# Matrix-LSTM key blocks: masks added in place on DMA-fetched row copies, DVE one block ahead of its own weighing

## The chip, the cores and the metric

The program runs on one core of one Trainium2 chip. The metric is the device time in microseconds (us), the median of several executions. The engines named below are PE (TensorE matmul), DVE (VectorE), ACT (ScalarE), POOL (GpSimd) and SP (SyncE); each has an instruction stream of its own and waits for the others by semaphores.

## What is computed

The reference is a transformer block with mixture of experts, then two layers with three mixers side by side (Fourier, matrix LSTM, latent attention) and an MLP. The change touches the matrix LSTM alone. The reference computes it by chunks with a running state:

```python
m_t = jnp.maximum(inter, dmat.max(axis=-1))
w_intra = jnp.exp(dmat - m_t[..., None])
s = jnp.einsum("bhtd,bhsd->bhts", qb, kb) * w_intra
num = jnp.einsum("bhts,bhsv->bhtv", s, vb) + ...
den = s.sum(axis=-1) + ...
h = num / jnp.maximum(jnp.abs(den), jnp.exp(-m_t))[..., None]
...
h = (h_f + h_b).transpose(0, 2, 1, 3)
h = h * lax.rsqrt(jnp.mean(h * h, axis=-1, keepdims=True) + EPS)
h = h.reshape(B, N, M_WIDTH) * g_m * jax.nn.sigmoid(mo)
```

There are 4 heads of width 96 and two directions. A sequence is 256 context tokens and 256 latent ones; layer 0 needs outputs for all 512, layer 1 for the 256 latent ones.

## The kernel before

The kernel does each head in full, without chunks: for head `h` and key block `kb` (0 to 3, 128 keys each), and both directions `d`, a 128 x n tile of weights is exp(row + mask + key bias), times q.k. The row (one number per query, `rows[d][:, 3]`, on 4 partitions, one per head) must first stand on all 128 partitions. The names:

- `spread(h, d)` (PE) copies the row of a head to 128 partitions of bank 6 by a matmul with 4 rows; ACT copies it to `rb[d]` in SBUF (L853).
- `args(h, kb)` (DVE, L2060) adds the causal mask to 256 columns of `rb[d]` and puts it into `arg[d]`; one such buffer for each direction, so it waits until the exps of the block before have read it (`ml_e`).
- `exps(h, kb)` (ACT, L843, L844, L846) puts the exps into `sq`, two buffers deep: it waits for `values` of two blocks before (`ml_v`).
- `keys(h, kb)` (PE) is q.k into bank 4 or 5; `weigh(h, kb)` (DVE, L2070) multiplies the exps by it, in place; `values(h, kb)` (PE) sums weights x v, with a column of ones for the denominator (row 96), over the four blocks.
- After block 3 of a head: `head_ln` (ACT, L817 and L820) takes ln|den| on one partition; `head_m` (PE) brings the row of maxima (`rows[d][:, 4]`) to partition 96; `head_min` (DVE, L2078); `head_exp` (ACT, L826) gives 1/den; `head_spread` (PE) puts it on 96 partitions by a matmul with one row; `head_sum` (DVE, L2085, L2086, L2088) copies it, multiplies and adds the directions (`quot`, semaphore `ml_sum`); `head_square` (ACT, L500), a matmul with ones (`norm`), `root` (ACT, L510 and L512), `head_value` (DVE, L2094, L2096), `head_round` (ACT) and `head_rest` (DVE, L1585) make the normed head and its high and low parts for the output projection.

Instruction order is written out by hand, per engine, as loops over `h` and `kb`; each engine runs its own list strictly in order. The tail steps of head h-1 stand among the blocks of head h. Ahead of the heads stand six roundings (`round_u`) on ACT and six `rest` on DVE for the parts of the other two mixers, and 16 copies on POOL (L451) that put the Fourier part on other partitions; they wait for the last of these `rest`. POOL also issues DMAs in order on a queue of its own (the modulation weights), SP those of the weight stream. After the heads PE runs the output projection: the first two output tiles go through k = 0 to 6 early, then wait for the last head (k = 7).

## Time and profile before

| | us |
|---|---|
| median of 3 executions | 1767.93 |
| lowest, highest | 1761.85, 1769.1 |
| profiled execution | 1768.98 |
| its span, first to last instruction | 1767.2 |
| matrix LSTM, layer 0 (end of attention to output tile k = 7) | 845.2 to 938.0 |
| matrix LSTM, layer 1 | 1482.0 to 1548.2 |

The profiled execution is one run; the span is 1.8 us shorter than its time. A row of the timeline is a start, a duration, the engine, the line and what it writes and reads. In a table of windows each row is a stretch, with the busy time of every engine in it and, after POOL, the granted clock of TensorE as a share of 2.4 GHz (0.50 is 1.2 GHz).

### The profile page before, as it was taken

The page shows a single profiled execution, that of the slowest core. Times are in us where ns is not written, and L with a number is a line of the kernel's source. Part 1 is how long each engine was busy: PE and PEld are TensorE (multiplying, and loading weights), DVE is VectorE, ACT ScalarE, POOL GpSimd, SP SyncE. Part 2 cuts the span into 40 slices and gives each one's busy share as a digit, 9 for nine tenths or more (in the row PEclk, how much of TensorE's full clock was granted, in tenths as well). Part 3 has the DMA queues.
Part 4 walks back from the last instruction along what each step waited for, and adds up shares of the span by engine and source line. Part 5 has one row for each costly group of instructions (what it writes and reads, how often), then busy time and mean ns, then how long its engine had stood idle before and what let it go on. Part 6 is the DMA issues. An engine that isn't in the chain of part 4 may idle for free.

```text
span 1767.2 us, 27194 instructions
## 1 busy us (share of the span) xinstructions
PE 1677.7 (95%) x9914; PEld 1398.0 (79%) x9914; DVE 1110.0 (63%) x1808; ACT 804.0 (45%) x1318; POOL 84.1 (5%) x140
## 2 busy tenths in 40 slices
PE   7999888999999999999899999999999998999997
PEld 7987477899999977766337788888887875589997
DVE  5544677768888888634665755555558835475564
ACT  5534444454444454344563542144225355566462
POOL 0000000000001000000200000000000001000000
PEclk9999899999999999999789999999999998799999
DMA  7634244357777732410003355455542420046562
GB/s 279 207 114 132 82 141 158 131 166 251 248 239 246 243 105 72 131 60 0 1 1 131 126 199 163 142 179 190 158 147 81 130 85 0 1 144 202 172 197 83
DMA packets 68921, 244.64 MB, mean 138 GB/s; under 512 B 7392, under 2 KB 10608, under 8 KB 68720
## 3 DMA queue, kind: packets, MB, share of 16 engines
q1 hardware_dynamic: 54000, 189.43, 32.2%
...
q8 instruction: 49, 0.80, 0.2%
...
## 4 chain that ended last, share of the span: by engine, by line
PE 80%; DVE 11%; ACT 5%; issue 3%; DMA 1%; DVEq 0%; SPq 0%; ACTq 0%
PE pair L948 79%; DVE uv L1596 1%; DVE wl L1556 1%; ACT wh L472 1%; DVE sq L1574 1%; DVE sq L1632 1%; PE pair L1116 1%; DVE small L1623 1%; DVE uh_f L1669 1%; ACT sq L500 1%; DVE ul L1585 1%; ACT sq L844 1%; ACT rstd L510 0%; ACT rstd L512 0%; ACT sq L542 0%
## 5 line engine op out<-in xcount | busy, mean ns | idle before, releaser
L948 PE MATMUL pair<-uh,wh 128*128 128x256 f32 (+3 forms) x1840 | 577.5, 314 | 16.1 <-DVE ul L1585 7.1
L1556 DVE TENSOR_TENSOR wl<-ring,wh 128x1024 fp32r<-128x1024 f32 x350 | 426.8, 1224 | 243.2 <-ACT wh L472 236.4
L948 PE MATMUL pair<-ul,wh 128*128 128x256 f32 (+3 forms) x1840 | 572.5, 311 | 0.0
L948 PE MATMUL pair<-uh,wl 128*128 128x256 f32 (+3 forms) x1840 | 572.2, 311 | 0.0
L472 ACT ACTIVATE wh<-ring 128x1024 fp32r<-128x1024 f32 x350 | 367.6, 1052 | 265.1 <-PE pair L948 261.4
L948 PEld LDWEIGHTS pair<-uh,wh 128*128 128x128 f32 (+1 forms) x1840 | 342.8, 186 | 50.8 <-issue 18.1
L948 PEld LDWEIGHTS pair<-uh,wl 128*128 128x128 f32 (+1 forms) x1840 | 342.9, 186 | 25.1
L948 PEld LDWEIGHTS pair<-ul,wh 128*128 128x128 f32 (+1 forms) x1840 | 342.7, 186 | 24.0
L948 PE MATMUL pair<-hh,wh 128*128 128x512 f32 (+1 forms) x512 | 172.6, 337 | 0.8
L948 PE MATMUL pair<-hl,wh 128*128 128x512 f32 (+1 forms) x512 | 172.0, 336 | 0.0
L948 PE MATMUL pair<-hh,wl 128*128 128x512 f32 (+1 forms) x512 | 172.0, 336 | 0.0
L948 PEld LDWEIGHTS pair<-hh,wh 128*128 128x128 f32 x512 | 97.1, 190 | 11.9 <-issue 2.0
L948 PEld LDWEIGHTS pair<-hh,wl 128*128 128x128 f32 x512 | 97.2, 190 | 10.1
L948 PEld LDWEIGHTS pair<-hl,wh 128*128 128x128 f32 x512 | 97.2, 190 | 9.9
L2194 DVE TENSOR_TENSOR hl<-sq,hh 128x512 f32 (+1 forms) x64 | 35.8, 559 | 93.9 <-ACT hh L907 93.8
L902 ACT ACTIVATE sq<-pair 128x512 f32<-128x512 f32 (+1 forms) x64 | 31.3, 489 | 105.4 <-PE pair L948 105.4
L948 PE MATMUL pair<-hidh,wl 128*128 128x256 f32 x256 | 72.6, 284 | 0.0
L948 PE MATMUL pair<-hidh,wh 128*128 128x256 f32 x256 | 72.5, 283 | 0.0
L948 PE MATMUL pair<-hidl,wh 128*128 128x256 f32 x256 | 72.4, 283 | 0.0
L992 PE MATMUL pair<-spin 128*128 128x512 f32 x260 | 66.9, 407 | 0.0
L948 PE MATMUL pair<-sq,table 128*128 128x256 f32 (+3 forms) x64 | 30.9, 594 | 31.4 <-DVE sq L1574 21.7
L948 PE MATMUL pair<-wh,uh 128*128 128x256 f32 (+1 forms) x192 | 57.1, 297 | 3.0 <-ACT qkp L734 3.0
...
## 6 DMA issues: line engine op xcount, KB each, us to landing
ring<-in_w_stream SPq DMA_DIRECT2D x350, 512.0 KB, 3.9
uh_f<-in_mods POOLq DMA_DIRECT2D x48, 512.0 KB, 6.1
mod_w<-in_mods POOLq DMA_DIRECT2D x48, 512.0 KB, 3.8
table<-in_table SPq DMA_DIRECT2D x1, 1849.5 KB, 12.4
...
res<-in_mem SPq DMA_DIRECT2D x1, 1024.0 KB, 14.7
res<-in_ctx POOLq DMA_DIRECT2D x1, 1024.0 KB, 6.3
uv<-c_rows POOLq DMA_DIRECT2D x2, 512.0 KB, 6.6
```

The costliest lines, as they stand in the source:

```text
L472: act.activation(wh[:, s, :], ring[:, s, :], ACT.Copy).then_inc(S("w_hi"), 1)
L500: act.activation(dst, src, ACT.Square).then_inc(S("norm_sq"), 1)
L844: last = act.activation(e[:, LAT], rb[d][:, LAT], ACT.Exp, bias=bias)
L902: act.activation(r, bank[(b0 + j) % 4][:, 0:n], ACT.Relu).then_inc(S("job_emptied_act"), 1)
L948: ins = pe.matmul(*operands, **flags)
L992: pe.matmul(bank[b], spin[:, 0:P], spin[:, :], start=True, stop=True)
L1116: last = pe.transpose(bank[6][:, to * P:(to + 1) * P], prob[i % 2][:, j * P:(j + 1) * P], ident)
L1556: tt(wl[:, s, :], ring[:, s, :], wh[:, s, :].bitcast(F32), ALU.subtract).then_inc(S("w_lo"), 1)
L1574: tt(sq[0:p, 3, 0:n], sq[0:p, 3, 0:n], sq[0:p, t % 2, 0:n], ALU.add).then_inc(S("norm_add"), 1)
L1585: last = tt(lo, v, hi.bitcast(F32), ALU.subtract)
L1596: last = stt(o, src, g, r, ALU.mult, ALU.mult)
L2194: tt(hl[:, d, 0:n].rearrange("p a b -> p (a b)"), sq[:, 2 + j % 2, 0:n], hh[:, d, 0:n].rearrange("p a b -> p (a b)").bitcast(F32), ALU.sub ...
```

## The change

It replaces `spread` and the ACT copy by DMAs, gives the row copies two buffers for each head parity, adds masks into the copies themselves, and reorders all four engines:

- POOL writes the rows of all heads to DRAM once (`ml_dram`) and reads the row of a head back with a broadcast to 128 partitions, twice, 512 KB each (`row_load`; copy 0 for key blocks 0 and 2, copy 1 for 1 and 3). The loads for heads 2 and 3 stand behind the 16 copies of POOL. `max_load` fetches the maxima in place of `head_m`.
- 1/den of heads 0 to 2 goes to DRAM and back with a broadcast (`den_spread`: a 4 KB write, a wait for it, a read of 384 KB; in layer 1 2 KB and 192 KB) in place of `head_spread`. Head 3 keeps the matmul (`last_spread`).
- `args` of the next block stands ahead of `weigh` of this one; `keys` of the next block ahead of `values` of this one.
- The two directions of a head step go in one instruction of 2 x n elements. exps of blocks 0 and 1 take 512 columns at once in layer 0.
- The six roundings and rests of the other mixers stand inside head 0. The norm of head h-2 stands in head h, where that of head h-1 stood.

DVE in layer 0, from the middle of head 1 to block 2 of head 2; `lw` and `ml` hold the row copies, `mo` is the gated head. Before:

```order
L2078 SCALAR_TENSOR_TENSOR ml<-ml,pair 1x512 x2
L2070 SCALAR_TENSOR_TENSOR sq<-pair,sq 128x512 x2
L2060 TENSOR_TENSOR ml<-ml,table 128x256 x2
L2085 COPY ml<-pair 96x512
L2086 TENSOR_TENSOR ml<-pair,ml 96x512
L2085 COPY ml<-pair 96x512
L2086 TENSOR_TENSOR ml<-pair,ml 96x512
L2088 TENSOR_TENSOR ml<-ml 96x512
L1585 TENSOR_TENSOR ul<-mo,uh 96x512
L2070 SCALAR_TENSOR_TENSOR sq<-pair,sq 128x256 x2
L2060 TENSOR_TENSOR ml<-ml,table 128x256 x2
L2070 SCALAR_TENSOR_TENSOR sq<-pair,sq 128x256 x2
```

and now, over the same heads:

```order
L2077 TENSOR_TENSOR lw<-lw,table 128x256 x2
L2087 SCALAR_TENSOR_TENSOR sq<-pair,sq 128x256 x2
L2105 TENSOR_TENSOR ml<-pair,ml 96x1024
L2106 TENSOR_TENSOR ml<-ml 96x512
L2077 TENSOR_TENSOR ml<-ml,table 128x256 x2
L2087 SCALAR_TENSOR_TENSOR sq<-pair,sq 128x512 x2
L2077 TENSOR_TENSOR lw<-lw,table 128x256 x2
L2087 SCALAR_TENSOR_TENSOR sq<-pair,sq 128x512 x2
L2112 SCALAR_TENSOR_TENSOR ml<-ml,table,rstd 96x512
L2114 TENSOR_TENSOR mo<-ml,mo 96x512
L2077 TENSOR_TENSOR ml<-ml,table 128x256 x2
L2094 SCALAR_TENSOR_TENSOR ml<-ml,mrow 1x1024
```

The pair of copies in `head_sum` (L2085) is gone, L2086 and L2078 are each one instruction (L2105, L2094), `head_sum` has moved from ahead of `weigh` of block 2 to behind `weigh` of block 3, and the norm's L2112 and L2114 now stand in the head after.

PE, layer 0, head 1 and the first block of head 2 (`qc` keys, `sq,mv` values, `rows_buf` and `ml` with `table` spreads, `sq,table` the norm). Before:

```order
L948 MATMUL pair<-rows_buf,table 128x512
L948 MATMUL pair<-qc 128x512
L948 MATMUL pair<-rows_buf,table 128x512
L948 MATMUL pair<-sq,mv 97x256 x2
L948 MATMUL pair<-qc 128x512
L948 MATMUL pair<-rows_buf,table 1x512 x2
L948 MATMUL pair<-sq,mv 97x512 x2
L948 MATMUL pair<-qc 128x256
L948 MATMUL pair<-ml,table 96x512 x2
L948 MATMUL pair<-sq,mv 97x512 x2
L948 MATMUL pair<-sq,table 96x512
L948 MATMUL pair<-qc 128x256
```

and now, from head 1 to the norm in head 2:

```order
L995 MATMUL pair<-qc 128x512
L995 MATMUL pair<-sq,mv 97x512 x2
L995 MATMUL pair<-qc 128x256
L995 MATMUL pair<-sq,mv 97x512 x2
L995 MATMUL pair<-qc 128x256
L995 MATMUL pair<-sq,mv 97x256 x2
L995 MATMUL pair<-qc 128x512
L995 MATMUL pair<-sq,mv 97x256 x2
L995 MATMUL pair<-qc 128x512
L995 MATMUL pair<-sq,mv 97x512 x2
L995 MATMUL pair<-sq,table 96x512
```

All small-row matmuls have left; the norm of head 0 comes behind the first `values` of head 2.

POOL, layer 0, from its last two copies on. Before:

```order
L451 COPY uh<-yfh 32x512
L451 COPY ul<-yfl 32x512
L432 DMA mod_c<-c_rows 128x1024 x2
L439 DMA mod_w_103<-in_mods 128x1024
L439 DMA mod_w_104<-in_mods 128x1024
```

and now:

```order
L497 COPY uh<-yfh 32x512
L497 COPY ul<-yfl 32x512
L457 DMA lw<-ml_dram 128x2x512
L457 DMA ml<-ml_dram 128x2x512
L472 DMA den_dram<-ml 16x1x64
L476 DMA ml<-den_dram 96x1024
L465 DMA mrow<-ml_dram 1x2x512
L457 DMA ml<-ml_dram 128x2x512 x2
L472 DMA den_dram<-ml 16x1x64
```

The loads for the next layer's modulation now stand behind the row loads of heads 2 and 3 and three pairs of a write of 1/den and its read, in one line.

The diff, its core:

```diff
-        rb, arg = [ml[:, d, :] for d in range(2)], [ml[:, 4 + d, :] for d in range(2)]
-        den, quot = [ml[MD:MD + 1, 2 + d, :] for d in range(2)], [ml[0:MD, 6 + d, :] for d in range(2)]
+        rb_even = [lw[:, 0:1024].rearrange("p (d t) -> p d t", d=2), ml[:, 0:2, :]]
+        rb = [rb_even, [ml[:, 2:4, :], ml[:, 4:6, :]]] * 2
+        mrow = mrow_at[MD:MD + 1]
+        den, quot = ml[MD:MD + 1, 6:8, :], ml[0:MD, 6:8, :]
...
+            def row_load(l, h, k):
+                if h >= 2:
+                    pool.wait_ge(S("ml_e"), 8 * (l * MH + h - 1))
+                pool.dma_start(rb[h][k], ml_dram[l, :, h, 0, :].rearrange("(o d) t -> o d t", o=1)
+                               .to_broadcast([P, 2, 512])).then_inc(S(f"rb_in{h}_{k}"), 16)
+            def max_load(l, h):
+                if h >= 2:
+                    pool.wait_ge(S("ml_min"), l * MH + h - 1)
+                k = 2 * (h % 2)
+                pool.dma_start(mrow[:, k:k + 2, :], ml_dram[l, :, h, 1, :].rearrange("(o d) t -> o d t", o=1)
+                               ).then_inc(S(f"max_in{h % 2}"), 16)
+            def den_spread(l, h):
+                out = den_dram[l, h, :, cols].rearrange("(o d) t -> o d t", o=1)
+                pool.wait_ge(S("ml_rden"), l * MH + h + 1)
+                pool.dma_start(out, den[:, :, cols]).then_inc(S("den_out"), 16)
+                pool.wait_ge(S("den_out"), 16 * (l * (MH - 1) + h + 1))
+                if h:
+                    pool.wait_ge(S("u_v"), value_count(f"y_{l}", MH + 2 + h - 1))
+                pool.dma_start(quot[:, :, cols], out.to_broadcast([MD, 2, cols.stop - cols.start])
+                               ).then_inc(S("quot_in"), 16)
             for l in range(NL):
                 cols = lin_cols(l)
+                for d in range(2):
+                    pool.wait_ge(S("ml_rows"), 2 * l + d + 1)
+                    pool.dma_start(ml_dram[l, d], rows[d][:, 3:5, :]).then_inc(S("rows_out"), 16)
+                pool.wait_ge(S("rows_out"), 32 * (l + 1))
+                pool.wait_ge(S("job_full"), JOBS.full(JOBS.number(f"va_{l}", 3)))
+                row_load(l, 0, 0)
+                for h in range(2):
+                    max_load(l, h)
+                pool.wait_ge(S("sm_s"), UNIT0["mlat1"] if l == 0 else len(UNITS))
+                pool.wait_ge(S("conv_done"), 8 * l + 8)
+                for h, k in ((0, 1), (1, 0), (1, 1)):
+                    row_load(l, h, k)
                 for j in range(2):
                     pool.wait_ge(S("u_l"), U_AT[f"y_{l}"] + MH + j + 1)
                     for q in range(4):
                         for dst, src in ((uh, yfh), (ul, yfl)):
                             pool.tensor_copy(dst[MD:P, 4 * j + q, cols],
                                              src[32 * q:32 * q + 32, j, cols]).then_inc(S("y_moved"), 1)
+                for h in range(MH - 1):
+                    if h + 2 < MH:
+                        for k in range(2):
+                            row_load(l, h + 2, k)
+                    den_spread(l, h)
+                    if h + 2 < MH:
+                        max_load(l, h + 2)
                 if l + 1 < NL:
                     pool.wait_ge(S("job_full"), JOBS.full(JOBS.number(f"out_{l}", 0)))
...
                 def head_ln(h):
                     act.wait_ge(S("ml_v"), 4 * (l * MH + h + 1))
-                    for d in range(2):
-                        b = bank[mlb(l, 2 * (h % 2) + d)]
-                        last = act.activation(den[d][:, cols], b[MD:MD + 1, cols], ACT.Abs)
-                    ch.link(last)
-                    for d in range(2):
-                        act.activation(den[d][:, cols], den[d][:, cols], ACT.Ln,
-                                       bias=table[MD:MD + 1, COL["tiny"][0]:COL["tiny"][0] + 1]).then_inc(S("ml_ln2"), 1)
+                    if h:
+                        act.wait_ge(S("den_out"), 16 * (l * (MH - 1) + h))
+                    ch.link(act.activation(den[:, :, cols], ml_pair(l, h)[MD:MD + 1, :, cols], ACT.Abs))
+                    act.activation(den[:, :, cols], den[:, :, cols], ACT.Ln,
+                                   bias=table[MD:MD + 1, COL["tiny"][0]:COL["tiny"][0] + 1]).then_inc(S("ml_ln2"), 1)
...
+                            act.wait_ge(S(f"rb_in{h}_{kb}"), 16 * (l + 1))
+                        if t >= 2:
+                            act.wait_ge(S("ml_v"), t - 1)
+                        act.activation(sq[:, 2 * (kb % 2) + d, c], rb[h][kb % 2][:, d, c], ACT.Exp,
+                                       bias=gcol[:, d, kb, h:h + 1]).then_inc(S("ml_e"), 1)
...
+                for h, kb in ML_STEPS:
+                    exps(h, kb)
+                    if h == 0 and kb < 3:
+                        round_y(2 * kb)
+                        round_y(2 * kb + 1)
+                    if kb == 0 and h >= 2:
+                        head_square(h - 2)
+                    if kb == 1 and h >= 2:
+                        head_root(h - 2)
+                    if kb == 1 and h:
                         head_ln(h - 1)
-                    if h >= 2:
+                    if kb == 2 and h:
+                        head_exp(h - 1)
...
+                head_square(MH - 2)
+                head_exp(MH - 1)
+                head_root(MH - 2)
                 head_round(MH - 2)
-                head_exp(MH - 1)
...
-                def spread(h, d):
-                    g = l * MH + h
-                    if d:
-                        pe.wait_ge(S("ml_b_in"), 2 * g + 1)
-                    elif g >= 2:
...
                 def keys(h, kb):
                     kk = 4 * (l * MH + h) + kb
...
+                def last_spread():
+                    pe.wait_ge(S("ml_rden"), (l + 1) * MH)
+                    pe.wait_ge(S("norm_rstd"), NORM[f"head_{l}_{MH - 2}"] + 1)
                     for d in range(2):
-                        mm(bank[7 - d][MD:MD + 1, cols], row_ident[d][:, h:h + 1], rows[d][:, 4, cols],
-                           start=True, stop=True).then_inc(S("ml_m"), 1)
-                def head_spread(h):
-                    for d in range(2):
-                        pe.wait_ge(S("ml_rden"), 2 * (l * MH + h) + d + 1)
-                        mm(bank[7 - d][0:MD, cols], ones[MD:MD + 1, 0:MD], den[d][:, cols],
-                           start=True, stop=True).then_inc(S("ml_bc"), 1)
-                for h in range(MH):
...
+                for j in range(4):
+                    claim(f"mlstm_{l}", j)
+                keys(0, 0)
+                for t, (h, kb) in enumerate(ML_STEPS):
+                    if t + 1 < len(ML_STEPS):
+                        keys(*ML_STEPS[t + 1])
+                    if kb == 0 and h >= 2:
+                        pe.wait_ge(S("ml_sum"), l * MH + h - 1)
+                    values(h, kb)
+                    if kb == 0 and h >= 2:
+                        head_norm(h - 2)
...
-                for k in range(4):
+                for k in range(KT - 1):
+                    if k == 4:
+                        head_norm(MH - 2)
+                    if k == 6:
+                        last_spread()
                     for m in range(2):
                         output(early[m], m, k)
-                head_spread(MH - 1)
...
                 def args(h, kb):
                     if kb < 2 and l:
                         return
+                    t = 4 * (l * MH + h) + kb
+                    c = CTX if kb < 2 else LAT
+                    a = rb[h][kb % 2]
+                    dve.wait_ge(S(f"rb_in{h}_{kb % 2}"), 16 * (l + 1))
                     for d in range(2):
-                        if kb == 0:
-                            dve.wait_ge(S("ml_b_in"), 2 * (l * MH + h) + d + 1)
-                        if kb:
-                            dve.wait_ge(S("ml_e"), 2 * (4 * (l * MH + h) + kb - 1) + d + 1)
-                        tc = CTX if kb < 2 else LAT
-                        tt(arg[d][:, tc], rb[d][:, tc], masks[d][:, kb % 2, :], ALU.add).then_inc(S("ml_arg"), 1)
+                        if kb >= 2:
+                            dve.wait_ge(S("ml_e"), 2 * (t - 2) + d + 1)
+                        tt(a[:, d, c], a[:, d, c], masks[d][:, kb % 2, :], ALU.add).then_inc(S("ml_arg"), 1)
                 def weigh(h, kb):
...
                 def head_min(h):
-                    for d in range(2):
-                        c = 2 * (l * MH + h) + d + 1
-                        dve.wait_ge(S("ml_ln2"), c)
-                        dve.wait_ge(S("ml_m"), c)
-                        stt(den[d][:, cols], den[d][:, cols], -1.0, bank[7 - d][MD:MD + 1, cols], ALU.mult,
-                            ALU.min).then_inc(S("ml_min"), 1)
+                    dve.wait_ge(S("ml_ln2"), l * MH + h + 1)
+                    dve.wait_ge(S(f"max_in{h % 2}"), 32 * l + 16 * (h // 2 + 1))
+                    k = 2 * (h % 2)
+                    stt(den[:, :, cols], den[:, :, cols], -1.0, mrow[:, k:k + 2, cols], ALU.mult,
+                        ALU.min).then_inc(S("ml_min"), 1)
                 def head_sum(h):
-                    for d in range(2):
-                        dve.wait_ge(S("ml_bc"), 2 * (l * MH + h) + d + 1)
-                        ch.link(dve.tensor_copy(quot[d][:, cols], bank[7 - d][0:MD, cols]))
-                        last = tt(quot[d][:, cols], bank[mlb(l, 2 * (h % 2) + d)][0:MD, cols], quot[d][:, cols], ALU.mult)
-                    ch.link(last)
-                    tt(quot[0][:, cols], quot[0][:, cols], quot[1][:, cols], ALU.add).then_inc(S("ml_sum"), 1)
+                    if h < MH - 1:
+                        dve.wait_ge(S("quot_in"), 16 * (l * (MH - 1) + h + 1))
+                    else:
+                        dve.wait_ge(S("ml_bc"), l + 1)
+                        ch.link(dve.tensor_copy(quot[:, :, cols],
+                                                pair[3][0:MD, :].rearrange("p (d t) -> p d t", d=2)[:, :, cols]))
+                    ch.link(tt(quot[:, :, cols], ml_pair(l, h)[0:MD, :, cols], quot[:, :, cols], ALU.mult))
+                    tt(quot[:, 0, cols], quot[:, 0, cols], quot[:, 1, cols], ALU.add).then_inc(S("ml_sum"), 1)
...
-                    args(h, 1)
-                    if h:
+                args(0, 0)
+                for t, (h, kb) in enumerate(ML_STEPS):
+                    if t + 1 < len(ML_STEPS):
+                        args(*ML_STEPS[t + 1])
+                    if kb == 2 and h:
                         head_min(h - 1)
-                    weigh(h, 1)
-                    args(h, 2)
-                    if h:
+                    weigh(h, kb)
+                    if h == 0 and kb < 3:
+                        rest_y(2 * kb)
+                        rest_y(2 * kb + 1)
+                    if kb == 1 and h >= 2:
+                        head_value(h - 2)
+                    if kb == 2 and h >= 2:
+                        head_rest(h - 2)
+                    if kb == 3 and h:
                         head_sum(h - 1)
-                    if h >= 2:
-                        head_rest(h - 2)
-                    weigh(h, 2)
-                    args(h, 3)
-                    weigh(h, 3)
-                    if h:
-                        head_value(h - 1)
                 head_min(MH - 1)
+                head_value(MH - 2)
                 head_rest(MH - 2)
```

## Rows read from the trace of the kernel before

**Rows 1.** The page: busy time, share of the span and instructions of each engine.

```profile
PE 1677.7 (95%) x9914; PEld 1398.0 (79%) x9914; DVE 1110.0 (63%) x1808; ACT 804.0 (45%) x1318; POOL 84.1 (5%) x140
```

**Rows 2.** Windows, cut at the ends of `head_sum`; columns in the first row.

```profile
core 0: us, PE busy (x) PEld busy (x) DVE busy (x) ACT busy (x) POOL busy (x), PEclk, DMA share, GB/s
845.20:874.30 29.10, 26.63 (x54) 9.15 (x54) 22.96 (x41) 17.24 (x35) 10.88 (x16) 0.80 0.00 1
874.30:895.10 20.80, 19.21 (x39) 6.90 (x38) 13.05 (x27) 12.42 (x24) 0.00 (x0) 0.75 0.00 0
895.10:914.70 19.60, 16.70 (x38) 5.96 (x38) 13.72 (x27) 12.42 (x24) 0.00 (x0) 0.85 0.00 1
914.70:938.00 23.30, 22.39 (x82) 13.74 (x80) 11.61 (x21) 10.42 (x17) 0.00 (x0) 0.95 0.00 0
1482.00:1501.20 19.20, 16.65 (x54) 9.28 (x54) 12.09 (x33) 10.94 (x28) 6.52 (x16) 0.81 0.00 1
1501.20:1518.70 17.50, 17.03 (x38) 8.95 (x38) 7.95 (x22) 8.26 (x20) 0.00 (x0) 0.50 0.00 0
1518.70:1531.50 12.80, 10.90 (x40) 5.91 (x38) 8.29 (x24) 8.26 (x20) 0.00 (x0) 0.90 0.01 2
1531.50:1548.20 16.70, 15.38 (x74) 10.99 (x74) 7.85 (x20) 7.12 (x17) 0.00 (x0) 0.80 0.00 0
```

**Rows 3.** Waits, layer 0: who waited for whom, us, times, longest.

```profile
ACT ml L853 <- PE pair L948: 9.8, 7, 2.2
DVE ml L2060 <- ACT ml L853: 7.5, 5, 1.7
```

**Rows 4.** Groups by shape, layer 0: busy us, mean ns, idle before.

```profile
L2060 DVE TENSOR_TENSOR ml<-ml,table 128x256 f32<-128x256 f32 x32 | 14.9, 498 | 7.5 <-ACT ml L853 7.5
L2070 DVE SCALAR_TENSOR_TENSOR sq<-pair,sq 128x512 f32<-128x512 f32 x16 | 11.0, 692 | 4.0 <-ACT sq L844 3.7
L2070 DVE SCALAR_TENSOR_TENSOR sq<-pair,sq 128x256 f32<-128x256 f32 x16 | 6.2, 418 | 4.6 <-PE pair L948 4.3
...
L820 ACT ACTIVATE ml<-ml,table 1x512 f32<-1x512 f32 x8 | 5.3, 708 | 0.1
...
L826 ACT ACTIVATE ml<-ml 1x512 f32<-1x512 f32 x8 | 4.6, 618 | 0.1
L817 ACT ACTIVATE ml<-pair 1x512 f32<-1x512 f32 x8 | 4.3, 582 | 1.1 <-PE pair L948 1.0
L510 ACT ACTIVATE rstd<-pair,table 96x512 f32<-96x512 f32 x4 | 2.7, 682 | 3.1 <-PE pair L948 3.1
```

**Rows 5.** Timeline, layer 0: start us, us, engine, line, what.

```profile
852.36 3.51 PE L948 MATMUL pair<-sq,mv 128*97 128x512 f32 x4 [1.97 <-DVE sq L2070]
...
866.90 1.96 PE L948 MATMUL pair<-sq,mv 128*97 128x512 f32 x4
...
875.03 2.02 PE L948 MATMUL pair<-sq,table 96*96 96x512 f32 x2 [0.63 <-ACT sq L500]
...
920.78 0.50 PE L948 MATMUL pair<-uh,wh 128*128 128x512 f32 x1
```

**Rows 6.** Timeline, layer 1, `values` and the norm at 1.2 GHz.

```profile
1512.52 2.02 PE L948 MATMUL pair<-sq,mv 128*97 128x256 f32 x4
...
1519.21 1.17 PE L948 MATMUL pair<-sq,table 96*96 96x256 f32 x2
```

**Rows 7.** The page: DMA issues, KB each, us from issue to landing.

```profile
res<-in_ctx POOLq DMA_DIRECT2D x1, 1024.0 KB, 6.3
...
mod_c<-c_rows POOLq DMA_DIRECT2D x2, 512.0 KB, 6.0
out_dram<-res SPq DMA_DIRECT2D x1, 1024.0 KB, 4.8
...
c_rows<-c_work POOLq DMA_DIRECT2D x1, 8.0 KB, 5.4
```

**Rows 8.** Instructions of `mod_w`, the 512 KB loads of POOL's queue.

```profile
DMA to landing us min/median/max: 3.6/3.8/10.4
```

122 lines of the change are left out of this document (38 added, 84 removed).

## The prediction

> **What bounds the kernel now.** Read first where the two matrix-LSTM stages lie: 845.2 to 938.0 us in layer 0 and 1482.0 to 1548.2 us in layer 1, together 159 us, 9% of the span; nothing else in the program changes. On the page PE is busy 95% of the span [rows 1], but that is an average over stages. The windows [rows 2] show the two stages, cut where each `head_sum` ends. No engine is full there: in the two middle windows of layer 0 DVE works 13.1 of 20.8 us and 13.7 of 19.6, ACT 12.4, and PE, whose records overlap and stretch, shows 19.2 and 16.7 at a granted clock of 0.75 and 0.85. So PE is at 1.2 GHz for 30 to 50% of the time, and in one window of layer 1 throughout (0.50). What sets the pace is a chain that passes between engines. The waits [rows 3] name its links: ACT waits 9.8 us for `spread`, DVE 7.5 us for ACT's copy of it. This is the part that the change takes away, so the question is which chain comes next.
>
> **What goes.** Per head PE loses two spreads, two one-row maxima matmuls and two one-row spreads of 1/den, ACT its two copies, DVE the two copies of `head_sum` (0.69 each in layer 0, a 512-column DVE operation [rows 4]). The blocks then flow: with `args` of the next block and `keys` of the next block ahead, one block needs two adds and two weighings on DVE, 0.8 + 1.4 us in a wide block of layer 0 [rows 4], and `values` runs beside that. I cost this part at nothing; it only has to be shorter than the chain below.
>
> **The chain that comes next.** Follow one head step in the new order, from the end of `head_sum`(h-2), time s, to the end of `head_sum`(h-1), layer 0:
> - `args` of block 1 (2 x 0.42, the 256-column DVE operation [rows 4]) and `weigh` of block 0 (2 x 0.69): 2.2.
> - `values` of block 0, then the norm of head h-2 behind it on PE. PE has just been idle for the whole wait below, so it is at 1.2 GHz: 3.5 and 2.0 [rows 5] (1.96 for these values at 2.4 GHz in the same rows). 5.5.
> - `root` on ACT: 0.68 and as much again less a little: 1.3 [rows 4]. Only behind it, in ACT's list, `head_ln`(h-1): on one partition, 1024 columns in place of twice 512 (0.58 and 0.71 each [rows 4]). Not in the trace; between once (1.3) and twice (2.6), taken 2.2. `head_value` (2 x 0.7) and the next `args` lie beside it on DVE.
> - `head_min` on 1024 columns: between 0.7 and 1.4, taken 1.25. `head_exp`: between 0.62 and 1.24 [rows 4], taken 1.1.
> - The round trip of 1/den: POOL writes 4 KB to DRAM, waits, reads 384 KB. Then `head_sum` of 1024 and 512 columns: 2.0. Eight handovers between engines, 0.3 in all.
>
> The round trip has no row. Its bounds: the shortest landing of a 512 KB load in POOL's queue is 3.6 us [rows 8], that of the 1024 KB store 4.8 [rows 7]; 512 KB more cost 1.2, so an empty transfer costs about 2.4, and 4 KB with 384 KB behind come to 2.4 + 3.3 = 5.7, with 0.2 for POOL's two starts 5.9. The other end is what the two nearest kinds took: 5.4 for the 8 KB write `c_rows` and 6.0 for the broadcast reads of it [rows 7], together 11.4. I take 5.9: the 5.4 was issued just behind the 1024 KB load that itself took 6.3, and the reads shared the queue with others, whereas the DMA share in all our windows is 0.00 or 0.01 [rows 2]. By the Trainium skill (page "DMA: Bandwidth & Descriptors", section on the anatomy of one DMA) a transfer from this queue costs about 2.0 us plus its bytes at 436 GB/s; 512 KB would then land in 3.2 us, and this trace has 3.6 to 3.8 [rows 8]. With the page's figures the round trip would be 5.1 us and the whole sum below about 4 us lower, 1772; the same page advises to issue a DMA early and wait for it late, and here the wait stands two steps behind the issue.
>
> Sum for layer 0: 2.2 + 5.5 + 1.3 + 2.2 + 1.25 + 1.1 + 5.9 + 2.0 + 0.3 = 21.75 us a head. DVE is through with `weigh` of block 3 at about s + 16.3, so of the round trip some 3.4 us show as idle DVE, and behind that wait stand `args` and `weigh` of the next head and so all of PE. Before, a head took 20.8 and 19.6 [rows 2]. Two heads: 43.5 against 40.4, **+3.1**.
>
> Layer 1 has half the columns: `weigh` 0.85, `values` 2.0 and norm 1.2 at 1.2 GHz [rows 6], `root` 0.85 (estimate, two thirds of 1.3), `head_value` with `args` 1.75 (now longer than the ln), min 0.7, exp 0.62 (one row of 512 columns now [rows 4]), round trip 2.4 + 2.85 + 0.2 = 5.4, `head_sum` 1.1, handovers 0.3: 14.75. Two heads 29.5 against 17.5 + 12.8 = 30.3, **-0.8**.
>
> **The start, up to `head_sum`(0).** The six rests no longer stand ahead of head 0: the first `weigh` comes 4 us earlier. But POOL's 16 copies wait for them, and they now start behind three blocks of head 0: in layer 0 at 845.2 + 3.6 (`weigh`) + 3.2 (four pairs of adds) + 3.4 (five rests of 0.69) = 855.4 us, in layer 1 at 1482.0 + 2.5 + 1.7 + 2.1 = 1488.3. They take 10.9 and 6.5 us [rows 2], and the row loads of head 2 and the write of 1/den stand behind them in POOL's line: issue at about 866.5 (855.4 + 10.9 and a little), two issues 1.1, the small write behind 1024 KB as `c_rows` was, 5.4, the read 3.3, `head_sum` 2.0 and a start of 0.1: 878.4 against 874.3, **+4.1**. Layer 1: 1494.5 + 1.1 + 5.4 + 2.85 + 1.2 = 1505.1 against 1501.2, **+3.9**.
>
> **The end, from `head_sum`(2) to the last k.** Before, PE had first to finish blocks and a maximum (output starts at 920.8 [rows 5], 6 us behind `head_sum`). Now it starts at once, but at 1.2 GHz after its wait, and the norm of head 2 stands behind k = 3 in it. Layer 0: 24 matmuls for k = 0 to 3, 5.5 at full clock (0.23 from start to start behind the row of 920.8 [rows 5]), 8.5 with a beginning at half clock; norm 1.05; root, k = 4 and 5 and the last spread 4.7; `head_sum`(3) 3.3; square 0.65, norm 1.05, root 1.35, value 1.45, round 0.65, rest 0.7: 23.4 against 23.3 [rows 2], **+0.1**. Layer 1, the same with half the columns: 5.0 + 0.65 + 2.7 + 1.85 + 0.45 + 0.65 + 0.9 + 0.9 + 0.9 = 14.0 against 16.7, **-2.7**.
>
> **Sum:** +3.1 - 0.8 + 4.1 + 3.9 + 0.1 - 2.7 = +7.7 us on the profiled execution's 1768.98, so 1776.7. That execution lies 1.05 above the median of the three, 1767.93; on the median's scale 1775.6, and I name **1776**. Changes under about 0.5%, 8.8 us, can hardly be told from none here, and the forecast is just at that bound.
>
> **Rivals.**
> - *Faster: the clock stays up.* The one-row and four-row matmuls are gone, and the windows with most of them are at 0.75 to 0.85. If PE's idle stretches don't cost it the clock, `values` and norm fall to 1.96 + 1.05 in layer 0 and about 1.1 + 0.65 in layer 1, -2.5 and -1.45 a head, twice each, and the ends lose 3.0 and 2.2: -13.1, 1763. Against it: a wait of 8 us a head on PE, where now a wait of 2.0 us stands ahead of the `values` that take 3.51 [rows 5]. If the round trip is short as well (both landings near 2), another 2 us a cycle go: 1755.
> - *Slower: the round trip costs what the nearest rows say.* At 11.4 it is 5.5 longer in two cycles of layer 0, 6.0 in two of layer 1, and the first reads are 2.7 and 3.1 longer: +28.8, 1805. From 2.5 us on the round trip is seen at all, at 4.3 the change breaks even, and each us above costs about 5. For it: DRAM written and read back at once, small pieces, a software queue. Against it: the queue is empty.
> - *It doesn't do what it says.* If the row loads land late, `args` wait for them and the old wait is back under a new name. They are issued 5 us or more ahead of need for heads 0, 1 and 3; for head 2 in layer 0 the copies hold them until 866.5, and they land near 871, still ahead of `head_sum`(0). No price of its own below 3 us of slip: 1776 to 1780.
>
> **Chances.** The forecast 0.50 (1768 to 1785, the bounds of ln, min, exp and one us of landing), the clock rival 0.22 (1755 to 1767), the long round trip 0.23 (1786 to 1805), late rows 0.05. The range that leaves 2 in 10 out: 1759 to 1798. Faster by over 0.5% (below 1759): 0.16, the lower half of the clock rival and what a walk of this kind overlooks. Within 0.5% (to 1776.8): the rest of it and 0.3 of the forecast, 0.38. Slower: 0.46.
>
> **What the profile of the changed kernel would show.** A head in layer 0 (between the two-direction additions of `head_sum`) near 21.8 us, in layer 1 near 14.8. DVE idle ahead of the 1024-column multiply of `head_sum`, released by a DMA, six times, 3 to 4 us each and longer at the first of a layer; no wait left ahead of `args`. The landings of the 1/den write near 2.4 (5.4 for the first of a layer) and of its read near 3.3. POOL's copies from about 855 to 866. The clock at 0.50 behind each of these waits. The forecast is wrong if the idle time in front of `head_sum` is under 2 us (then faster), if the landings are 5 us and more (then slower), or if PE keeps 1.00 through the waits.

## The result, and the profile after

The changed kernel takes 1775.59 us (median of 8 runs, 1773.87 to 1783.25), the kernel before in the same comparison 1768.13 (8 runs). The two medians differ by 7.5 us; the measured ratio is 1.0058, with a 95% interval of 1.0038 to 1.0077, so the change is slower by about 10 us (7 to 14). I had forecast 1776. The total came out right, in part by luck: of its six terms, four were too high by 3.7 us together and two too low by 7.0, as worked out below.

The windows of the profiled execution, cut as in [rows 2], at the ends of `head_sum`. Columns: stretch, its length, busy us (and instructions) of PE, PEld, DVE, ACT and POOL, the granted clock, DMA share, GB/s.

```profile
843.90:880.80 36.90, 21.08 (x52) 9.02 (x52) 21.82 (x45) 16.42 (x27) 17.55 (x23) 0.82 0.31 71
880.80:901.80 21.00, 14.51 (x26) 5.82 (x26) 11.78 (x24) 10.05 (x15) 1.57 (x3) 0.66 0.18 46
901.80:922.50 20.70, 11.09 (x22) 4.65 (x22) 11.07 (x20) 10.87 (x15) 1.04 (x2) 0.66 0.06 19
922.50:945.60 23.10, 21.26 (x66) 13.95 (x66) 8.59 (x10) 7.03 (x10) 0.00 (x0) 0.78 0.00 1
1488.50:1515.00 26.50, 12.75 (x52) 8.35 (x52) 12.89 (x35) 11.73 (x27) 11.58 (x23) 0.83 0.32 82
1515.00:1529.10 14.10, 9.63 (x26) 6.50 (x26) 7.23 (x19) 7.06 (x15) 1.70 (x3) 0.72 0.31 69
1529.10:1543.10 14.00, 7.07 (x22) 4.51 (x22) 7.34 (x20) 7.46 (x16) 1.19 (x2) 0.88 0.04 14
1543.10:1556.90 13.80, 12.04 (x58) 10.30 (x59) 5.04 (x10) 4.52 (x10) 0.00 (x0) 0.76 0.01 2
```

Against [rows 2] the two middle windows of layer 0 hold less work (DVE 11.8 and 11.1 us, before 13.1 and 13.7) and are still no shorter; in the first windows POOL works 17.6 and 11.6 us, before 10.9 and 6.5, and they are 7.8 and 7.3 us longer. The clock in the middle windows of layer 0 fell from 0.75 and 0.85 to 0.66.

The start of layer 0, POOL and DVE in the timeline (start, duration, engine, line, what; in brackets the idle time before and what ended it). `lw<-ml_dram` is the row load for head 2, L472 the write of 1/den, L476 its read, L2105 the multiply of `head_sum`(0):

```profile
866.39 0.71 POOL L457 DMA_DIRECT2D lw<-ml_dram  x1
867.09 0.72 POOL L457 DMA_DIRECT2D ml<-ml_dram  x1
867.80 0.53 POOL L472 DMA_DIRECT2D den_dram<-ml  x1
872.33 0.76 DVE L2077 TENSOR_TENSOR lw<-lw,table 128x256 f32<-128x256 f32 x2 [9.82 <-DMA lw<-ml_dram]
...
875.35 0.55 POOL L476 DMA_DIRECT2D ml<-den_dram  x1 [7.01 <-DMA den_dram<-ml]
...
878.88 1.22 DVE L2105 TENSOR_TENSOR ml<-pair,ml 96x1024 f32<-96x1024 f32 x1 [5.12 <-DMA ml<-den_dram]
```

DVE is idle for 9.8 us ahead of `args` of head 2, which waits for a row load, and for 5.1 more ahead of the multiply. POOL waits 7.0 us for its write of 4 KB before it can issue the read.

One head step in layer 0, from the end of `head_sum`(1) at 901.79 to that of `head_sum`(2) at 922.48, the links of the chain:

```profile
903.80 3.70 PE L995 MATMUL pair<-sq,mv 128*97 128x512 f32 x4 [3.12 <-DVE sq L2087]
...
907.30 1.67 PE L995 MATMUL pair<-sq,table 96*96 96x512 f32 x2
...
909.01 0.68 ACT L563 ACTIVATE rstd<-pair,table 96x512 f32<-96x512 f32 x1 [5.33 <-PE pair L995]
...
910.38 1.02 ACT L871 ACTIVATE ml<-pair 1x1024 f32<-1x1024 f32 x1
910.38 0.75 DVE L2112 SCALAR_TENSOR_TENSOR ml<-ml,table,rstd 96x512 f32<-96x512 f32 x1 [4.86 <-ACT rstd L565]
...
912.60 1.22 DVE L2094 SCALAR_TENSOR_TENSOR ml<-ml,mrow 1x1024 f32<-1x1024 f32 x1
...
913.86 1.05 ACT L877 ACTIVATE ml<-ml 1x1024 f32<-1x1024 f32 x1 [0.36 <-DVE ml L2094]
...
915.20 0.53 POOL L472 DMA_DIRECT2D den_dram<-ml  x1 [17.79 <-ACT ml L877]
...
917.07 0.51 POOL L476 DMA_DIRECT2D ml<-den_dram  x1 [1.34 <-DMA den_dram<-ml]
...
920.53 1.22 DVE L2105 TENSOR_TENSOR ml<-pair,ml 96x1024 f32<-96x1024 f32 x1 [3.58 <-DMA ml<-den_dram]
```

This is the chain of the prediction, link by link: `args` and `weigh` to 903.8, `values` 3.5 us at half clock (903.80 to 907.30; 1.96 in [rows 5]), the norm, `root`, ln to 912.6, minimum, exp, the round trip from 915.20 to 920.53 = 5.3, the sum to 922.48.

### The profile page after: what moved, and what is told of

It is laid out like the page before. It is cut to its first block, busy times and chain, and to the rows that moved or that the text cites. A ratio compares the mean times of both kernels' runs of the same rounds, so it can differ in the third digit from the quotient of the medians.

```text
span 1776.6 us, 27000 instructions
## 1 busy us (share of the span) xinstructions
PE 1643.2 (92%) x9826; PEld 1390.2 (78%) x9826; DVE 1098.5 (62%) x1778; ACT 789.9 (44%) x1262; POOL 111.4 (6%) x180
## 4 chain that ended last, share of the span: by engine, by line
PE 76%; DVE 11%; issue 6%; ACT 4%; POOL 2%; DMA 2%; DVEq 0%; SPq 0%; ACTq 0%; POOLq 0%
PE pair L995 75%; DMA den_dram<-ml 1%; DVE wl L1570 1%; DVE uv L1610 1%; ACT wh L525 1%; DVE sq L1588 1%; PE pair L1163 1%; DVE sq L1646 1%; POOL uh L497 1%; DVE small L1637 1%; DVE uh_f L1683 1%; PE pair L1039 1%; POOL ul L497 1%; DVE ul L1599 1%; ACT sq L553 0%
## 5 line engine op out<-in xcount | busy, mean ns | idle before, releaser
L995 PE MATMUL pair<-sq,mv 128*97 128x256 f32 (+1 forms) x128 | 51.3, 532 | 49.9 <-DVE sq L2087 49.7
L995 PEld LDWEIGHTS pair<-sq,mv 128*97 128x97 f32 x128 | 22.7, 196 | 75.3 <-DVE sq L2087 38.4
L1039 PE MATMUL pair<-spin 128*128 128x512 f32 x260 | 72.3, 432 | 0.0
## 6 DMA issues: line engine op xcount, KB each, us to landing
table<-in_table SPq DMA_DIRECT2D x1, 1849.5 KB, 12.9
```

The costliest lines, as they stand in the source:

```text
L995: ins = pe.matmul(*operands, **flags)
L1039: pe.matmul(bank[b], spin[:, 0:P], spin[:, :], start=True, stop=True)
```

## The experiments

All stage times that follow are of the two matrix-LSTM stages alone, in the profiled execution, each from the end of the last attention copy to the end of the last `head_rest`; a stage is cut at the ends of the addition of `head_sum` (L2106 in the changed kernel). "First" is the first section, from the start of the stage to `head_sum`(0); the next three are the steps from one `head_sum` to the next. The first two of them are the middle steps; the third has no round trip, since head 3 keeps the matmul. The last column is the measured ratio to the kernel before, beside runs of before on the same chip. The stages are the better measure of the two: ahead of them the eleven profiled executions differ by up to 9.6 us (layer 0 starts between 839.4 and 849.0), while the middle steps of layer 0 are 21.0, 21.3 and 21.1, then 20.7, 20.9 and 20.9, in the changed kernel and the two runs that move only work at the start. Line numbers shift a little from kernel to kernel.

| kernel | layer 0: first, steps, stage | layer 1: first, steps, stage | both | ratio (95%) |
|---|---|---|---|---|
| before | 29.1, 20.8 19.6 16.4, 92.7 | 19.1, 17.5 12.8 12.6, 66.1 | 158.8 | 1 |
| after | 36.9, 21.0 20.7 16.0, 101.6 | 26.4, 14.2 13.9 9.7, 68.4 | 170.0 | 1.0058 (1.0038 to 1.0077) |
| copies_late | 26.1, 21.3 20.9 16.1, 91.4 | 19.2, 17.7 14.0 10.3, 65.2 | 156.6 | 0.9973 (0.9956 to 0.9989) |
| rows_early | 30.0, 21.1 20.9 16.0, 95.0 | 20.9, 14.0 14.2 9.6, 63.2 | 158.2 | 1.0005 (0.9989 to 1.0020) |
| chain_first | 36.3, 15.3 15.0 14.6, 88.2 | 26.8, 10.5 9.0 8.2, 58.5 | 146.7 | 0.9938 (0.9916 to 0.9959) |
| write_twice | 38.5, 21.7 22.6 17.0, 105.9 | 28.8, 15.8 16.4 10.4, 75.5 | 181.4 | 1.0133 (1.0106 to 1.0160) |
| pe_spread | 32.9, 20.9 18.5 16.0, 95.3 | 16.5, 14.7 11.4 9.4, 56.5 | 151.8 | 0.9934 (0.9912 to 0.9957) |
| warm | 36.6, 18.4 19.1 16.4, 97.6 | 26.7, 12.9 12.8 9.7, 66.5 | 164.1 | 1.0036 (1.0018 to 1.0055) |
| late_first | 24.1, 22.4 16.1 16.2, 84.9 | 19.1, 17.3 10.6 8.2, 59.7 | 144.6 | 0.9926 (0.9901 to 0.9951) |
| pe_first | 26.0, 17.2 16.1 16.8, 82.2 | 17.6, 10.6 11.6 8.2, 52.1 | 134.3 | 0.9857 (0.9828 to 0.9887) |
| woven | 24.3, 16.0 15.2 14.6, 77.0 | 19.8, 12.1 10.4 8.2, 54.5 | 131.5 | 0.9849 (0.9823 to 0.9875) |

Taken as differences from the changed kernel, the column "both" and the ratio agree within 4 us for every row (woven: 131.5 less 170.0 is -38.5 us; 0.9849 less 1.0058, times 1768, is -37).

### The start: POOL's order

`copies_late` puts the 16 copies behind the first round trip:

```diff
                 for h in range(MH - 1):
                     if h + 2 < MH:
                         for k in range(2):
                             row_load(l, h + 2, k)
                     den_spread(l, h)
                     if h + 2 < MH:
                         max_load(l, h + 2)
+                    if h == 0:
+                        ...
```

(the copies stood ahead of this loop).

> The changed kernel with one thing moved: POOL's 16 copies of a layer stand behind the loads for head 2 and the round trip of 1/den of head 0, not ahead of them. Theory (the start of each layer is held by POOL's order): 1/den of head 0 is ready at 862.8 us in the trace of the changed kernel and is written only at 867.8, behind two 512 KB loads; with the copies behind it the write goes out at about 863.1 and lands in 1.9, the read lands 3.5 later, and head_sum(0) ends near 870.5 instead of 880.8 (-10), in layer 1 near 1507.5 instead of 1515.0 (-7.5); later heads unchanged. In all 1776 - 18 = 1758. Rival (the loads of head 2 themselves are slow beside the weight stream, in whatever place they stand): the wait for them stays, at most 5 us are won, 1771 or more. Second rival: the copies now collide with head 2 and hold the write of head 1: the cycle of head 1 grows by 3 to 5 us, 1763 to 1768.

The write left when 1/den was ready, and both starts moved as expected, -10.8 and -7.2 us. The stages together lost 13.4 us and not 18. POOL in layer 0 and, for the second round trip, in layer 1:

```profile
857.89 0.53 POOL L472 DMA_DIRECT2D den_dram<-ml  x1 [7.79 <-ACT ml L878]
859.79 0.54 POOL L476 DMA_DIRECT2D ml<-den_dram  x1 [1.37 <-DMA den_dram<-ml]
...
1496.84 1.46 POOL L457 DMA_DIRECT2D ml<-ml_dram  x2
1500.47 0.53 POOL L472 DMA_DIRECT2D den_dram<-ml  x1 [2.17 <-ACT ml L878]
1505.95 0.66 POOL L476 DMA_DIRECT2D ml<-den_dram  x1 [4.96 <-DMA den_dram<-ml]
```

In layer 1 the second rival is there too: the copies pushed the two loads for head 3 to 1496.8, the next write got in behind them and took 5.5 us to the read instead of 1.8, and that step is 17.7 us instead of 14.2: this is most of what is missing from the 18.

`rows_early` separates the effect of the copies from that of the queue: the two loads for head 2 go ahead of the copies, the write stays behind them.

```diff
+                for k in range(2):
+                    row_load(l, 2, k)
                 for j in range(2):
                     ...
                 for h in range(MH - 1):
-                    if h + 2 < MH:
+                    if h == 1:
                         for k in range(2):
                             row_load(l, h + 2, k)
                     den_spread(l, h)
```

> The changed kernel with one thing moved: only the two loads for head 2 stand ahead of POOL's 16 copies; the write of 1/den stays behind the copies, but with nothing queued in front of it. It parts the start's delay into the copies and the queue. Theory (in the changed kernel the small write is slow, 7.3 us, because it stands behind 1 MB of loads in POOL's DMA queue, and those loads come late as well): the write goes out at 866.4 on the scale of the changed kernel's trace, lands in 1.9, the read in 3.5, head_sum(0) ends near 873.8 (-7) in layer 0 and near 1508.4 (-6.5) in layer 1: 1776 - 13.5 = 1762. Rival (a first write after a pause is slow by itself): the landing stays near 7 us and head_sum(0) moves by less than 2 us, 1773 or more. Second rival (the copies are what holds, the queue is cheap): -3 a layer, 1770.

```profile
862.12 0.53 POOL L472 DMA_DIRECT2D den_dram<-ml  x1
864.00 0.54 POOL L476 DMA_DIRECT2D ml<-den_dram  x1 [1.35 <-DMA den_dram<-ml]
```

The same write, at the same place behind the copies, is now 1.9 us from issue to issue of the read, where it was 7.5. The first sections lose 6.9 and 5.5 us (7 and 6.5 expected). So the first write after a long pause isn't slow by itself; the 1 MB ahead of it in the queue is what makes it slow. It isn't DVE's work either: in the changed kernel DVE idles from 862.5 to 872.3, and the write was issued at 867.8. Between this run and `copies_late` lie 3.9 and 1.7 us: that is what the copies' own place costs.

All the traces together say when such a write is through. In the changed kernel, `copies_late`, `chain_first`, `write_twice`, `late_first` and `woven`, POOL's next instruction goes out 8.7 to 9.5 us after the issue of the first of two 512 KB loads, whether the write left 1.4 us behind that issue (and took 7.3 to 8.0 us), 3.6 (5.5), 5.3 (4.1, `woven`, layer 1) or 6.3 (2.5, `copies_late`, layer 1); where it left 7.9 us behind it or more, the write took its own 1.9 (858.58 to 860.47 in `woven`). So the write seems to be through only when the loads ahead of it are, which land 5.0 to 8.4 us after their issue in the changed kernel. Whether the order in the queue or the shared DMA engines cause this, no run separates.

### The head step: round trip, order, clock

`write_twice` lengthens each round trip by one more small write.

> The changed kernel with 1/den written to DRAM twice, one write behind the landing of the other, which makes each of the six round trips longer by one small write (1.9 us from issue to the next issue in the trace). Theory (each us of the round trip costs a us, since DVE waits for it six times): six times 1.9, +11, 1787; by the prediction's own slope of 5 per us, +9.4. Rival (the end of the round trip only looks like the last thing, the engines have other slack): under +3, 1776 to 1779.

```diff
-                pool.dma_start(out, den[:, :, cols]).then_inc(S("den_out"), 16)
-                pool.wait_ge(S("den_out"), 16 * (l * (MH - 1) + h + 1))
+                for k in range(2):
+                    pool.dma_start(out, den[:, :, cols]).then_inc(S("den_out"), 16)
+                    pool.wait_ge(S("den_out"), 32 * (l * (MH - 1) + h) + 16 * (k + 1))
```

```profile
887.44 1.02 PE L996 MATMUL pair<-sq,table 96*96 96x512 f32 x2
...
894.69 0.53 POOL L473 DMA_DIRECT2D den_dram<-ml  x1 [15.64 <-ACT ml L878]
896.57 0.51 POOL L473 DMA_DIRECT2D den_dram<-ml  x1 [1.35 <-DMA den_dram<-ml]
898.44 0.52 POOL L477 DMA_DIRECT2D ml<-den_dram  x1 [1.36 <-DMA den_dram<-ml]
```

Each extra write is 1.9 us, and the stages grow by 11.4: 11.4 / 1.88 = 6.1 us for each us of round trip. The six sections that hold a round trip grow by 10.8 of these, where six full writes are 11.3; on the whole the round trips are seen in full, and the rival is out. One by one they are less even, 0.7 to 2.5 us. The 0.7 is the first middle step of layer 0, and there something else got faster: the norm behind `values` took 1.02 us (the first line above) instead of 1.91 in the changed kernel, at full clock instead of half.

`chain_first` leaves the round trip as it is and moves what stands ahead of it:

```diff
 ACT:
+                    if kb == 0 and h:
+                        head_ln(h - 1)
                     if kb == 0 and h >= 2:
                         head_square(h - 2)
+                    if kb == 1 and h:
+                        head_exp(h - 1)
                     if kb == 1 and h >= 2:
                         head_root(h - 2)
-                    if kb == 1 and h:
-                        head_ln(h - 1)
-                    if kb == 2 and h:
-                        head_exp(h - 1)
 DVE:
-                    if kb == 2 and h:
-                        head_min(h - 1)
                     weigh(h, kb)
+                    if kb == 0 and h:
+                        head_min(h - 1)
```

> The changed kernel with another order on ACT and DVE alone: ln, minimum and exp of head h-1 stand ahead of root and value of head h-2 (ln and minimum in block 0, exp in block 1), so that 1/den is written to DRAM about 8 us earlier and the round trip of 5.3 us lies beside the norm. Theory (the chain norm, root, ln, minimum, exp, round trip sets a head, and its order is the cause): the 3.0 to 3.7 us of idle DVE ahead of the sum's multiply vanish in the two middle heads of each layer, L0 cycle near 17.7 instead of 20.8, L1 near 10.6 instead of 14.0: -6 and -7, in all 1776 - 13 = 1763. The first heads stay held by POOL. Rival (the engines' work sets the head, about 18 us of DVE and PE in layer 0, and the wait only moves to the value and the weighings): less than 1 us a head, 1772 to 1776.

The middle steps of layer 0 fell by 5.7 us, not 3, those of layer 1 by 3.7 and 4.9; the first sections didn't move (36.3 and 26.8), since POOL holds them. One step in layer 0:

```profile
887.20 1.22 DVE L2094 SCALAR_TENSOR_TENSOR ml<-ml,mrow 1x1024 f32<-1x1024 f32 x1
...
888.46 1.05 ACT L877 ACTIVATE ml<-ml 1x1024 f32<-1x1024 f32 x1 [1.27 <-DVE ml L2094]
...
889.80 0.53 POOL L472 DMA_DIRECT2D den_dram<-ml  x1 [7.41 <-ACT ml L877]
...
893.00 0.75 DVE L2112 SCALAR_TENSOR_TENSOR ml<-ml,table,rstd 96x512 f32<-96x512 f32 x1 [2.59 <-ACT rstd L565]
...
895.03 0.54 POOL L476 DMA_DIRECT2D ml<-den_dram  x1 [4.70 <-DVE mo L2114]
...
898.63 1.22 DVE L2105 TENSOR_TENSOR ml<-pair,ml 96x1024 f32<-96x1024 f32 x1 [0.88 <-DMA ml<-den_dram]
```

The write goes out 4.5 us after `head_sum`(0) (ends 885.30; 13.7 in the same step of the changed kernel), and lies beside the norm. The read now waits for `head_value`, which frees `quot`, and of the whole round trip 0.9 us are seen. The gain of 5.7 us is larger than the vanished wait, and the two traces say where it comes from. The idle time of DVE ahead of the multiply gives 2.1 (2.95 less 0.88). The stretch from `head_value` to the last weighing gives 2.5 (4.7 us instead of 7.2): ln and minimum, 3.4 us together, had stood behind the wait for `root`, ahead of the exps and the weighing of block 2, and held the blocks as well; they now fill time in which ACT and DVE waited for PE. The remaining 1.1 is the clock, not the order of the chain: `values` and the norm took 4.3 us instead of 5.4, the norm 1.02 instead of 1.91.

`pe_spread` drops the DRAM way: for every head two one-row matmuls into banks 6 and 7 behind `values` of block 2, and the DVE copy, as the last head has them; `den_spread` is gone from POOL.

> The changed kernel without the round trip through DRAM: 1/den of every head is spread by two one-row matmuls and a DVE copy out of PSUM (1.2 us in layer 0, 0.7 in layer 1), as the last head's already is. Theory (the round trip is seen in full where DVE waits): middle heads -2 us each in layer 0 (3.3 of idle time less 1.2 for the copy) and -2.8 each in layer 1; at the start of a layer 1/den no longer waits for POOL, only the loads of head 2 do: -4 and -6. In all 1776 - 19 = 1757. Rival (the two one-row matmuls and the copy cost what the wait cost, since PE comes out of an idle stretch at 1.2 GHz): middle heads unchanged, 1766. Second rival (the round trip is hidden and what ends last is something else): 1776 or more.

```diff
                     values(h, kb)
                     if kb == 0 and h >= 2:
                         head_norm(h - 2)
+                    if kb == 2 and h:
+                        head_spread(h - 1)
```

```profile
896.91 1.93 PE L994 MATMUL pair<-sq,mv 128*97 128x512 f32 x4 [0.24 <-DVE sq L2089]
...
904.58 1.05 ACT L876 ACTIVATE ml<-ml 1x1024 f32<-1x1024 f32 x1 [0.35 <-DVE ml L2096]
...
906.42 3.72 PE L994 MATMUL pair<-ml,table 1*96 1x512 f32 x4
...
910.18 1.22 DVE L2102 COPY ml<-pair 96x1024 f32<-96x1024 f32 x1 [2.51 <-PE pair L994]
...
1498.04 0.91 ACT L896 ACTIVATE sq<-lw,gcol 128x256 f32<-128x256 f32 x2 [6.12 <-DMA lw<-ml_dram]
```

The total is near what was expected (-18.2 us, -19 expected), but not where: the first middle step of each layer didn't gain (20.9 and 14.7), the second did (-2.2 and -2.5), the starts gained 4.0 and 9.9. The first rival holds for layer 0: the two spreads take 3.7 us at half clock, and DVE still idles 2.5 us ahead of the copy. From the end of exp to the multiply PE's way takes 6.7 and 5.8 us in the two middle steps, the way through DRAM 5.7 and 5.6. That the second step is 2.2 us shorter all the same comes from the clock: PE waited less, so `values` and the norm took 1.93 + 1.02 us instead of 3.50 + 1.67. In layer 1 PE's way is the shorter one (3.1 and 4.0 us against 5.4 and 5.2), but the first middle step gains nothing by it, since the row load for head 2 comes too late: ACT waits 6.1 us for it (the last line above). So the late rows, which the round trip hides in the changed kernel, are the next thing that holds the start and, in layer 1, the step behind it.

`warm` puts filler matmuls into PE's wait ahead of `values` of heads 2 and 3.

> The changed kernel with filler matmuls of 512 columns on PE, into a bank that nothing uses there, ahead of the wait for head_sum that stands before values of heads 2 and 3: 22 and 12 of them in layer 0, 48 and 10 in layer 1, to fill about 90% of the idle time that the trace of the changed kernel shows there. Theory (the granted clock is 0.5 in values and norm because PE idled just before, and both lie on the path): values and norm fall from 3.5 + 1.7 to about 2.0 + 1.0 us in two heads of layer 0 and from 2.0 + 1.1 to 1.1 + 0.65 in two of layer 1, and the heads get shorter by as much: -2.2 x 2 and -1.3 x 2, in all 1776 - 7 = 1769. Rival (the clock is not on the path, since DVE's two weighings and args lie beside values): under 2 us. Second rival (the fillers delay keys or values): 1778 or more.

```diff
                     if kb == 0 and h >= 2:
+                        turn_over({(0, 2): 22, (0, 3): 12, (1, 2): 48, (1, 3): 10}[l, h], 6)
                         pe.wait_ge(S("ml_sum"), l * MH + h - 1)
```

```profile
882.65 2.43 PE L1039 MATMUL pair<-spin 128*128 128x512 f32 x10
884.93 1.93 PE L995 MATMUL pair<-sq,mv 128*97 128x512 f32 x4
886.69 1.02 PE L995 MATMUL pair<-sq,table 96*96 96x512 f32 x2
```

`values` fell from 3.5 to 1.9 us and the norm from 1.7 to 1.0, and the four middle steps by 2.6, 1.6, 1.3 and 1.1 = 6.6 (7 expected). The half clock lies on the chain. In the whole program less is left: the stages are 5.9 us shorter, and the ratio is 1.0036 against 1.0058, about 4 us; those two intervals overlap, so that the gain in the stages is shown by the trace and the gain in the whole is not.

### Put together

`late_first` is `copies_late` and `chain_first` at once.

> Both reorderings at once: POOL's copies behind the first round trip, and ln, minimum and exp ahead of root and value. Theory (start and cycle are separate terms that add up): the runs of each alone gave the sections 13 and 23 us less than the changed kernel; together -36, 1776 - 36 = 1740, with head_sum(0) at 26 us from the start of the stage in layer 0 (36.9 before) and cycles near 15 and 10. Rival (now the copies lie where the write of head 1's 1/den comes due, 8 us earlier than in the run with the copies moved alone, and hold it): the first cycle of each layer is 4 to 6 us longer than with the other order alone, 1748 to 1752.

The rival won, and at a higher price than it had named: the starts and the later steps added up, but the first middle steps came to 22.4 and 17.3 us, 7 us more than with the other order alone (4 to 6 expected), since the write of head 1 is now due some 9 us earlier and meets the copies and the 1 MB for head 3:

```profile
876.22 1.48 POOL L457 DMA_DIRECT2D ml<-ml_dram  x2
877.69 0.53 POOL L472 DMA_DIRECT2D den_dram<-ml  x1
885.73 0.54 POOL L476 DMA_DIRECT2D ml<-den_dram  x1 [7.52 <-DMA den_dram<-ml]
```

`pe_first` is the same with the spreads of `pe_spread`.

> As the run with both reorderings, but 1/den is spread by PE and copied by DVE in every head, with no round trip. Theory (with the chain ahead the round trip is hidden, so PE's way can only cost its copy): middle heads 1 us longer than with both reorderings, the first heads 2 to 4 us shorter; 1738 to 1742, the same within 0.3%. Rival (the round trip still ends last): 1732 or less.

It came to 0.9857, 1742 us: the level that was expected, but from the wrong comparison, since `late_first` itself was slower than expected, 1754 us. The first sections came to +1.9 and -1.5 us against `late_first`, where 2 to 4 us less were expected. What it tells is that without a round trip POOL's copies hold nobody (17.2 and 10.6 in the steps that were 22.4 and 17.3).

`woven` keeps the round trip and cuts the copies (`copies(j, quarters)` is the old loop over part j):

```diff
+                for k in range(2):
+                    row_load(l, 2, k)
+                den_spread(l, 0)
+                max_load(l, 2)
+                copies(0, (0, 1))
+                for k in range(2):
+                    row_load(l, 3, k)
+                copies(0, (2, 3))
+                den_spread(l, 1)
+                max_load(l, 3)
+                copies(1, range(4))
+                den_spread(l, 2)
```

> Both reorderings (ln, minimum and exp ahead; POOL's copies behind the first round trip), with the copies cut in three: four behind the first round trip, then the loads for head 3, four more, the round trip of head 1, the last eight. Theory (with both reorderings the first cycle of a layer was 22.4 and 17.3 us because the write of head 1 stood behind all 16 copies and behind the 1 MB for head 3): the first cycles come to 15 to 17 in layer 0 and 10 to 12 in layer 1, all else as with both reorderings, 1754 - 12 = 1742. Rival (in that run head 1 was held by something other than POOL): the first cycles stay above 20 and 15, 1750 or more.

```profile
863.90 1.48 POOL L457 DMA_DIRECT2D ml<-ml_dram  x2
...
871.14 0.53 POOL L472 DMA_DIRECT2D den_dram<-ml  x1 [2.45 <-ACT ml L883]
876.25 0.54 POOL L476 DMA_DIRECT2D ml<-den_dram  x1 [4.58 <-DVE mo L2120]
```

The first load is issued 7.2 us ahead of the write, the write waits for ACT and no longer for POOL, and the first middle steps are 16.0 and 12.1 us. At 0.9849 (1737.39 us, 6 runs) it is 1.5% faster than the kernel before and 2.1% faster than the changed one (0.9849 / 1.0058 = 0.979); `pe_first` can't be told from it. Filler matmuls on top of it were not tried.

## Why the prediction was right, and where its steps were off

The steps, predicted and measured, in us. The starts are counted from the start of each stage: predicted 878.4 - 845.2 = 33.2 and 1505.1 - 1482.0 = 23.1.

| step | predicted | measured |
|---|---|---|
| layer 0, middle step | 21.75 | 21.0, 20.7 |
| layer 1, middle step | 14.75 | 14.2, 13.9 |
| layer 0, start to `head_sum`(0) | 33.2 | 36.9 |
| layer 1, start to `head_sum`(0) | 23.1 | 26.4 |
| layer 0, end to the last k | 23.4 | 23.1 |
| layer 1, end | 14.0 | 13.8 |
| both stages against before | +7.7 | +11.2 |

**The chain of the head step** is right in every link, and `write_twice`, `chain_first` and `warm` show by three different moves that it is the chain that sets the middle steps. In layer 0 the steps came out 0.8 and 1.1 us shorter than forecast, and most of that is the round trip: 5.9 predicted, 5.3 measured (write 1.9 from issue to issue, read 3.5). In layer 1 5.1 and 4.9 against 5.4. The lower of the two bounds was the good one; the price by the Trainium skill (page "DMA: Bandwidth & Descriptors", section on the anatomy of one DMA), an estimate of 5.1, was nearer than mine. The upper bound, the rival's 11.4, had taken the `c_rows` write for the price of a small write. It was the price of a small write behind a large load: the first of each layer here, 7.5 and 7.3 us to the read's issue, looks like it, the other four don't.

**The start** is the term that was mis-sized, by 3.7 and 3.3 us. In layer 0 the copies began 1.3 us earlier after the stage's start than I had them (852.88 - 843.94 = 8.9, not 10.2), but took 13.5 us instead of 11.1 (+2.4); the issues 1.4 instead of 1.1; the write behind 1 MB 7.5 instead of 5.4 (+2.1); the read 3.5 instead of 3.3. In layer 1 the copies cost 1.2 more, the write 1.9 more. The mechanism, POOL's order, is as predicted, and `copies_late` and `rows_early` show it. (My sum for layer 1 also carried a slip of 0.3: 1488.3 + 6.5 is 1494.8, not 1494.5.)

**The rival of late rows** had a chance of 0.05, and I expected "no wait left ahead of `args`". That is wrong for head 2 in layer 0: DVE waited 9.8 us for its row load. The load landed at 872.3, ahead of `head_sum`(0) as I had it, but `args` of head 2 stand ahead of `head_sum`(0) in DVE's list, and so the wait was there. It cost little of its own, since the round trip ended later still. `pe_spread`, without the round trip, shows what lay behind it: the start still took 32.9 us, against 26.1 in `copies_late`, where the rows come early.

**The slope** of "about 5" us for each us of round trip above 4.3 is 6.1 over the stages and 5.7 over the six sections with a round trip, mostly because the two first round trips count in full as well (+1.6 and +2.4 us for an extra write of 1.9).

**The clock.** It was at 0.50 in `values` behind the waits, as predicted, and they took 3.5 us. But the wait ahead of them was 5.3 and 3.1 us in the middle steps of layer 0, not the 8 us that I had held against the rival. So the rival that the clock stays up fell, and `warm` priced it: 6.6 us on the four steps, where I had 2 x (2.5 + 1.45) = 7.9.

**What the total hides.** The steps and the ends were 3.7 us too high, the starts 7.0 too low; in the stages together +11.2 came where +7.7 was forecast. That the median says 1776 to within 0.4 us is luck. The forecast stood on the profiled execution, 1776.7 on that scale, and this one took 1778.91. Its rest outside the stages was 1.8 us shorter than before (span +9.4, stages +11.2), which is less than that part differs from one profiled execution to the next.

What I had missed altogether is that the order was the lever: the prediction names `head_ln` "only behind" `root` in ACT's list as a fact of the chain, and had not asked what the same work costs in another order.
